# Router logits of six token tiles, computed with the router's weights stationary in four column groups

## The chip, the cores and the metric

The kernel runs on one core of a Trainium2 chip. Its engines are TensorE (PE, matrix products and transposes), VectorE (DVE), ScalarE (ACT), GpSimd (POOL) and SyncE (SP, which issues DMAs). Each runs its own instruction stream in order; they wait for each other with semaphores. The metric is device time in microseconds of one execution. A product here is written out = lhsT^T x rhs: the stationary operand lhsT (at most 128 rows by 128 columns) is loaded into PE's array, the moving operand rhs streams through, one column after another. All products in question are float32; the trace shows each as two records of MATMUL and two of LDWEIGHTS.

## What is computed

One decoder block on 1024 tokens of width 1024: a norm, a joint projection, differential attention (4 heads) beside a chunkwise mLSTM (4 heads), an output projection, then a mixture of 32 experts with 4 chosen per token, and a last norm. The part that matters:

```python
x = x + mixed @ w_out[l]
# moe(rms_norm(x, norm_ffn_g[l]), ...):
logits = (xt @ router_w + router_b).astype(jnp.float32)      # xt: 1024 x 1024, router_w: 1024 x 32
top_val, top_idx = lax.top_k(logits, TOP_K)
gates = jax.nn.softmax(top_val, axis=-1)
```

## The kernel before

The 1024 tokens are cut into NT = 8 tiles of P = 128 rows, the depth of 1024 into KD = 8 slices of 128. The kernel has three stages: the projections with the mLSTM (to some 395 us), the attention stage (to some 640 us), and the experts (a loop over 32 items with their weights streamed in, to the end).

The attention stage is a software pipeline written out by hand. A unit u = 4t + h is one head h of one tile t (N_UNITS = 32). Each engine runs a loop over u, and each of its steps holds pieces of several units:

- PE, step u: da_turn_weights(u-2, 0), the transposes of the attention weights of unit u-2 (L813); da_logit(u), the scores of unit u (L791); further transposes da_turn_weights(u-2, 1) where the tile has more than four blocks; a piece that depends on u % 4; da_values(u-2), the products with the values (L824). The piece is, with t = u//4 - 2: for u % 4 = 0 the first half of the output projection of tile t (out_project, L851), then place(t-1); for 1 its second half; for 2 turn_x1(t), the transposes of the new rows (L860); for 3 route(t), the router's logits (L870), then da_turn(t+1) (L832).
- DVE, step u: for u % 4 = 0 first da_mix(t) (L1551) and choose(t-1), which reads the logits (L1593) and picks four experts; for 1 residual (L1565), scale_rows and slots; for 3 take_h2T(t) and da_norm. Then da_combine(u-1), which joins the two exponentials of unit u-1, and da_softmax_in(u), which takes the scores of unit u out of PSUM with their maximum (L1522, L1525).
- ACT, step u: the copies of unit u-2's transposed weights out of PSUM (L1212), then pieces by u % 4, then da_exps(u), two exponentials (L1192).

da_logit(u) waits for da_max of unit u-1, that is for DVE's softmax_in(u-1), because it overwrites the banks that this reads. The PSUM banks of the pieces are dealt out in turn from a ring of two (5 and 7) by next_bank; a piece waits until the bank's last user has been read ("logits" by choose's first instruction, through logits_read).

route(t) computes 128 tokens x 32 experts: for each of the eight depth slices the 128x128 slice of h2T (the turned rows of the tile) is stationary and the 128x32 slice of the router's weights rw streams. Line 870:

```python
ins = pe.matmul(ps[:, 0:N_EXP], h2T[t % 2][:, k, :], rw[:, k, :], start=(k == 0), stop=(k == KD - 1))
```

Tiles 6 and 7 (NT-2, NT-1) are routed after the pipeline, between the last output projections. no_rows is a 128x160 tile of one constant, which POOL writes and sends to list_dram early (list_clear counts these two DMAs); nothing uses it later. The gate rows of the first stage (L659 and L664) are two products of 36 stationary columns each, into PSUM partitions 0 to 35 and 64 to 99.

Of the kernel before, what the change touches and what calls it, by code (L numbers as in the profile page):

```python
# [23 lines left out]
F32 = mybir.dt.float32  # L24
# [62 lines left out]
def build(nc, x, norm_attn_g, w_in, rel_bias_table, lambda_q1, lambda_k1, lambda_q2, lambda_k2,  # L87
# [18 lines left out]
    with ExitStack() as ctx:  # L106
# [20 lines left out]
        def kn(t, k=KD):  # L127
# [105 lines left out]
        no_rows = sb("no_rows", [P, 160], I32)  # L233
        x_idx = unit[3][:, 3136:3136 + N_EXP * LISTS].bitcast(I32)
# [13 lines left out]
         log_f_part, em_in, em_ready, cols_ps, cols_ready, wide_ps, wide_ready,  # L248
# [4 lines left out]
             "cols_ps", "cols_ready", "wide_ps", "wide_ready", "dve_step", "act_step",  # L253
# [34 lines left out]
        ident_ready, table_in, gate_w_in, lam_in_sem, router_in, squared, gain_rows_in, ml_divided, \  # L288
            ml_squared, da_squared, sum_squared = (sem(n) for n in (
            "ident_ready", "table_in", "gate_w_in", "lambda_in", "router_in", "squared",  # L290
# [4 lines left out]
        out_sent, wide_out = sem("out_sent"), sem("wide_out")  # L295
        spot_ready, last_summed = sem("spot_ready"), sem("last_summed")
# [48 lines left out]
        N_SMALL = 6 + 4  # L345
# [123 lines left out]
        def _(pool):  # L469
# [23 lines left out]
            for half in range(2):  # L493
# [4 lines left out]
                               pattern=[[1, P]], channel_multiplier=-1).then_inc(consts, 1)  # L498
            for n in range(NT):
                pool.wait_ge(mean_sq, NT + n + 1)  # L500
                pool.tensor_tensor(small[:, 4:8], small[:, 0:4], neg_half[:, 0:4], ALU.pow).then_inc(rstd_ready, 1)
# [128 lines left out]
        def _(pe):  # L630
# [50 lines left out]
            pe.wait_ge(table_in, 32)  # L681
# [182 lines left out]
            def route(t):  # L864
                pe.wait_ge(h2T_ready, 2 * t + 2)
                if t == 0:
                    pe.wait_ge(router_in, 32)
                ps = next_bank("logits", t)
                for k in range(KD):
                    ins = pe.matmul(ps[:, 0:N_EXP], h2T[t % 2][:, k, :], rw[:, k, :], start=(k == 0), stop=(k == KD - 1))  # L870
                ins.then_inc(logits_done, 1)
# [26 lines left out]
            for u in range(2, N_UNITS + 2):  # L898
                t = u // 4 - 2
                da_turn_weights(u - 2, 0)  # L900
                if u == 2:
                    ml_turn(NT - 1, next_bank("ml", NT - 1))
                if u < N_UNITS:
                    da_logit(u)
                if u + 1 < LATE_V:
                    late_values(u + 1)
                if len(da_groups[u - 2]) > 1:
                    da_turn_weights(u - 2, 1)
                if u in (6, 8):
                    turn_biases((u - 6) // 2)  # L910
                if u % 4 == 0 and t >= 0:
                    out_project(t, 0)
                    if t >= 1:
                        place(t - 1)
                if u % 4 == 1 and 0 <= t < NT - 2:
                    out_project(t, 1)
                if u % 4 == 2 and t >= 0:
                    turn_x1(t, 0)
                    turn_x1(t, 1)
                if u % 4 == 3 and t >= -1:  # L920
                    if t >= 0:
                        route(t)
                    da_turn(t + 1)
                da_values(u - 2)
# [136 lines left out]
        def _(act):  # L1061
# [22 lines left out]
            act.dma_start(table[:, :], rel_bias_table).then_inc(table_in, 16)  # L1084
            act.dma_start(one_hot, buckets).then_inc(table_in, 16)
# [120 lines left out]

            g = 0
            for u in range(len(da_units) + 2):
# [17 lines left out]
                if u % DAH == 1 and u > DAH:  # L1226
# [6 lines left out]
                    for h in range(DAH):  # L1233
                        act.activation(da_sq[:, h, :], da_o[:, h, :], ACT.Square,
                                       accum_out=small[:, h:h + 1]).then_inc(da_squared, 1)

# [73 lines left out]
        def _(dve):  # L1310
# [274 lines left out]
            def choose(t):  # L1585
# [7 lines left out]
                dve.scalar_tensor_tensor(out=lg[:, :], in0=bank(ring_bank["logits", t])[:, 0:N_EXP], scalar=rstd[:, t:t + 1],  # L1593
# [341 lines left out]
```

## Time and profile before

| what | us |
|---|---|
| median of 3 runs (lowest to highest) | 2265.82 (2259.61 to 2268.32) |
| the profiled execution | 2265.43 |
| its span, first to last instruction | 2263.6 |
| PE busy | 2192.9 |
| DVE busy | 1413.0 |
| ACT busy | 565.9 |
| POOL busy | 258.3 |

The durations below come from the profiled execution. A row of the timeline merges successive records of one form: start, time from the first start to the last end, engine, line, operation, and in brackets the idle time ahead and what ended it. The chain of the work that ended last follows the span back from its last instruction; where an engine worked without waiting, it stays on that engine.

### The profile page before, as it was taken

Reading aid. Unit: us, or ns where it says so; the run is one execution under the profiler, and the core shown is the slowest. Engines: PE = TensorE matmul, PEld = TensorE weight load, DVE = VectorE, ACT = ScalarE, POOL = GpSimd, SP = SyncE. Lnnn points to the kernel's source line nnn. Section 1 sums busy time; section 2 is a strip of 40 time slices with the busy share of each in tenths; the row PEclk is TensorE's granted clock in tenths of the full one; section 3 lists DMA queues with packets and bytes.
Section 4 is the critical chain, followed back from the end, with each engine's and each line's share of the span. In section 5 each row is a group of like instructions: output and inputs, shape, how many; then the busy total and the mean of one; then the engine's idle time right before and its main releaser. Section 6 shows DMA issues by size and latency. Waiting matters only on the chain.

```text
span 2263.6 us, 40201 instructions
## 1 busy us (share of the span) xinstructions
PE 2192.9 (97%) x14677; PEld 1893.8 (84%) x14679; DVE 1413.0 (62%) x2880; ACT 565.9 (25%) x1240; POOL 258.3 (11%) x235
## 2 busy tenths in 40 slices
PE   8999999999978999999999999999999999999996
PEld 4444554566668999999999999999999999999996
DVE  3352231678684777777778677764755566667567
ACT  2122221344311222222222222321221122222123
POOL 1000000121230110111001000110100000001013
PEclk9999999999988999999999999999999999999998
DMA  8000011210165899989989888976976788788688
GB/s 312 34 38 0 0 38 40 98 58 29 67 210 175 282 306 306 304 283 307 312 277 311 282 282 305 311 256 210 304 262 224 235 278 286 244 294 295 232 257 294
DMA packets 244662, 488.92 MB, mean 216 GB/s; under 512 B 24572, under 2 KB 24780, under 8 KB 244452
## 3 DMA queue, kind: packets, MB, share of 16 engines
q1 hardware_dynamic: 223684, 452.48, 57.3%
q0 software_dynamic: 20704, 35.60, 7.1%
q8 instruction: 34, 0.56, 0.1%
q10 hardware_dynamic: 224, 0.16, 0.0%
q14 instruction: 16, 0.13, 0.0%
HBM read 477.67 MB, written 49.63 MB: 233 GB/s over the span
## 4 chain that ended last, share of the span: by engine, by line
PE 92%; DVE 4%; issue 1%; ACT 1%; DMA 1%; POOL 0%; DVEq 0%; SPq 0%; POOLq 0%; ACTq 0%
PE PS L1024 66%; PE PS L664 15%; PE PS L851 5%; PE PS L791 1%; PE PS L824 1%; DVE pairA L1793 1%; PE PS L813 1%; PE PS L870 0%; DMA pairB<-acc_dram 0%; DVE unit L1522 0%; DVE pairA L1839 0%; PE PS L736 0%; DVE unit L1833 0%; PE PS L659 0%; PE PS L637 0%
## 5 line engine op out<-in xcount | busy, mean ns | idle before, releaser
L1024 PE MATMUL PS<-pairA,unit 128*128 x12288 | 1563.1, 290 | 31.3 <-DVE pairA L1839 11.9
L1024 PEld LDWEIGHTS PS<-pairA,unit 128*128 128x128 f32 x12288 | 1554.5, 191 | 40.0 <-issue 39.4
L1774 DVE STREAM_TRANSPOSE unit<-unit 32x512 f32<-32x512 f32 (+1 forms) x512 | 325.5, 636 | 10.3 <-DMA unit<-h_dram,cur_x 3.0
L1793 DVE STREAM_TRANSPOSE pairA<-unit 32x512 f32<-32x512 f32 (+1 forms) x512 | 325.8, 636 | 7.1
L664 PE MATMUL PS<-pairA,unit 128*128 128x512 f32 (+1 forms) x528 | 231.1, 594 | 1.4 <-issue 1.4
L1276 ACT ACTIVATE unit<-PS,cur_b 128x256 f32<-128x256 f32 x256 | 107.5, 471 | 414.9 <-PE PS L1024 414.9
L560 POOL DMA_INDIRECT unit<-h_dram,cur_x x66 | 68.8, 1042 | 1184.4 <-DVE cur_x L1829 1160.5
L664 PEld LDWEIGHTS PS<-pairA,unit 128*128 128x128 f32 (+1 forms) x528 | 97.4, 188 | 116.1 <-issue 115.4
L1259 ACT ACTIVATE unit<-unit 128x512 f32<-128x512 f32 x128 | 80.6, 630 | 453.8 <-DVE unit L1821 453.8
L1265 ACT ACTIVATE unit<-PS,cur_b 128x256 f32<-128x256 f32 x256 | 107.4, 471 | 317.7 <-PE PS L1024 314.2
L1813 DVE COPY cur_b<-b_all 128x24 f32 x32 | 6.7, 209 | 265.2 <-ACT unit L1276 261.3
L1836 DVE TENSOR_SCALAR unit<-unit 128x512 f32<-128x512 f32 x128 | 54.5, 426 | 167.0 <-ACT unit L1265 164.1
L1821 DVE TENSOR_SCALAR unit<-PS,cur_b 128x256 f32<-128x256 f32 x256 | 108.7, 478 | 40.7 <-PE PS L1024 38.6
L581 POOL DMA_INDIRECT acc_dram<-pairA,cur_y x64 | 102.8, 1606 | 211.4 <-ACT pairA L1251 201.0
L664 PE MATMUL PS<-unit,pairA 128*128 128x512 f32 x256 | 112.0, 595 | 0.3 <-ACT unit L1115 0.3
L664 PEld LDWEIGHTS PS<-unit,pairA 128*128 128x128 f32 x256 | 48.0, 190 | 59.5 <-issue 58.2
L1833 DVE TENSOR_TENSOR unit<-unit 128x512 f32<-128x512 f32 x128 | 88.4, 691 | 8.8
L1839 DVE SCALAR_TENSOR_TENSOR pairA<-unit 128x512 f32<-128x512 f32 x128 | 88.7, 693 | 4.4
L1251 ACT ACTIVATE pairA<-pairA,g_now 128x512 f32<-128x512 f32 x128 | 81.6, 715 | 1.8 <-DVE pairA L1793 1.8
L1782 DVE TENSOR_TENSOR pairA<-unit,vec 128x448 f32<-128x448 f32 x128 | 71.4, 620 | 0.0
L1522 DVE CUSTOM_DVE_ANT_0 unit<-PS,unit 128x128 f32<-128x128 f32 (+7 forms) x64 | 48.0, 750 | 29.2 <-PE PS L791 29.2
L1192 ACT ACTIVATE unit<-unit,small 128x128 f32<-128x128 f32 (+7 forms) x64 | 49.4, 772 | 51.5 <-DVE small L1525 51.0
(252 smaller groups left out, 1130.6 us busy)
## 6 DMA issues: line engine op xcount, KB each, us to landing
unit<-in_expert_w_gu_dram SPq DMA_DIRECT2D x256, 1024.0 KB, 5.1
unit<-in_expert_w_down_dram SPq DMA_DIRECT2D x128, 1024.0 KB, 8.2
unit<-in_w_in_dram SPq DMA_DIRECT2D x6, 2048.0 KB, 15.9
pairB<-in_x_dram SPq DMA_DIRECT2D x16, 512.0 KB, 5.9
unit<-in_w_out_dram SPq DMA_DIRECT2D x2, 2048.0 KB, 8.9
h_dram<-pairA SPq DMA_DIRECT2D x8, 512.0 KB, 2.6
acc_dram<-pairB SPq DMA_DIRECT2D x8, 512.0 KB
pairB<-acc_dram SPq DMA_DIRECT2D x8, 512.0 KB, 7.9
```

What stands on the lines that cost most here:

```text
L581: pool.indirect_dma_start(out=acc_dram, out_offset=bass.IndirectOffsetOnAxis(ap=cur_y[:, b:b + 1], axis=0), in_=y_rows[:, b, :], in_offset ...
L664: ins = pe.matmul(ps, lhs, rhs, start=(k == 0), stop=(k == KD - 1))
L851: ins = pe.matmul(ps, (da_mixT, ml_mixT)[k // 4][:, k % 4, P * t:P * t + P], w_o[k // 4][:, k % 4, HALF * half:HALF * half + HALF], start= ...
L1024: ins = pe.matmul(ps[:, ITEM * (j % 2):ITEM * (j % 2) + w], slot_w[s][:, k, P * j:P * j + P], xa_cols[:, ITEM * kd:ITEM * kd + KD * ITEM + ...
L1251: act.activation(half, half, ACT.Identity, scale=g_now[:, q // 2, :]).then_inc(y_evac, 1)
L1265: ins = act.activation(lin_b[:, b, ITEM * j:ITEM * j + ITEM], bank(2 + b)[:, ITEM * j:ITEM * j + ITEM], ACT.Identity, bias=cur_b[:, f:f + 1])
L1276: ins = act.activation(yT[:, 2 * s + j, :], bank(s)[:, ITEM * j:ITEM * j + ITEM], ACT.Identity, bias=cur_b[:, 2 * NF + 2 * s + j:2 * NF + ...
L1774: ins = dve.transpose(cols[:, :, :, 32 * q:32 * q + 32], rows[:, :, :, 32 * a:32 * a + 32])
L1793: ins = dve.transpose(rows[:, :, :, 32 * a:32 * a + 32], cols[:, :, :, 32 * q:32 * q + 32])
L1821: ins = dve.tensor_scalar(glu_t[:, b, ITEM * j:ITEM * j + ITEM], bank(b)[:, ITEM * j:ITEM * j + ITEM], cur_b[:, f:f + 1], LIMIT, ALU.add, ...
L1833: step.do(dve.tensor_tensor(glu_s[:, b, :], glu_t[:, b, :], glu_s[:, b, :], ALU.mult))
L1839: dve.scalar_tensor_tensor(out=actT[:, 2 * c:2 * c + 2, :].rearrange("p j n -> p (j n)"), in0=lin_c[:, b, :], scalar=1.0, in1=glu_s[:, b, ...
```

## The change

For tiles 0 to 5, route(t) exchanges the operands. The router's slice rw[:, k, :] (128x32) is now stationary, h2T[:, k, :] (128x128) streams, and the result is turned: 32 experts x 128 tokens. The eight slices go to four column groups of the array: group q (PSUM partitions 32q to 32q+31) sums slices 2q and 2q+1. So a bank holds four partial sums one below the other, 128x128 in all. ACT copies them to SBUF (take_parts, at the end of its step u = 4t + 11, behind da_exps(u)), into a part of no_rows. PE then makes one product (sum_logits, in step u = 4t + 12 between da_turn_weights(u-2, 0) and da_logit(u)): the partial sums are stationary, and a 128x32 matrix fold of four identities one below the other streams, which adds the four parts and turns the result back to tokens x experts. It goes to columns 128 to 159 of the same bank, where choose reads it. POOL makes fold after the matrix `above`. Tiles 6 and 7 stay as they were. Besides, the two loads of the bias table count to small_in rather than to a semaphore of their own, and an unused semaphore is dropped.

```diff
+        logit_parts, fold = no_rows[:, 0:P].bitcast(F32), sb("fold", [P, N_EXP])
...
-        N_SMALL = 6 + 4
+        N_SMALL = 6 + 4 + 2
...
+            step.do(pool.memset(fold[:, :], 0.0))
+            for q in range(4):
+                ins = pool.affine_select(out=fold[:, :], in_=fold[:, :], compare_op=ALU.not_equal, fill=1.0, base=-32 * q,
+                                         pattern=[[-1, N_EXP]], channel_multiplier=1)
+                if q < 3:
+                    step.do(ins)
+            ins.then_inc(consts, 1)
...
-            pe.wait_ge(table_in, 32)
...
-                for k in range(KD):
-                    ins = pe.matmul(ps[:, 0:N_EXP], h2T[t % 2][:, k, :], rw[:, k, :], start=(k == 0), stop=(k == KD - 1))
-                ins.then_inc(logits_done, 1)
+                if t >= NT - 2:
+                    for k in range(KD):
+                        ins = pe.matmul(ps[:, 0:N_EXP], h2T[t % 2][:, k, :], rw[:, k, :], start=(k == 0), stop=(k == KD - 1))
+                    ins.then_inc(logits_done, 1)
+                    return
+                for j in range(2):
+                    for q in range(4):
+                        ins = pe.matmul(ps[32 * q:32 * q + 32, 0:P], rw[:, 2 * q + j, :], h2T[t % 2][:, 2 * q + j, :],
+                                        start=(j == 0), stop=(j == 1))
+                ins.then_inc(parts_done, 1)
+
+            def sum_logits(t):
+
+                if t == 0:
+                    pe.wait_ge(consts, 6)
+                pe.wait_ge(parts_ready, t + 1)
+                pe.matmul(bank(ring_bank["logits", t])[:, P:P + N_EXP], logit_parts, fold[:, :],
+                          start=True, stop=True).then_inc(logits_done, 1)
...
+                if u % 4 == 0 and t >= 1:
+                    sum_logits(t - 1)
...
-            act.dma_start(table[:, :], rel_bias_table).then_inc(table_in, 16)
-            act.dma_start(one_hot, buckets).then_inc(table_in, 16)
+            act.dma_start(table[:, :], rel_bias_table).then_inc(small_in, 16)
+            act.dma_start(one_hot, buckets).then_inc(small_in, 16)
...
+            def take_parts(t):
+                if t == 0:
+                    act.wait_ge(list_clear, 32)
+                else:
+                    act.wait_ge(logits_done, t)
+                act.wait_ge(parts_done, t + 1)
+                act.activation(logit_parts, bank(ring_bank["logits", t])[:, 0:P], ACT.Copy).then_inc(parts_ready, 1)
...
+                if u % 4 == 3 and u >= 11:
+                    take_parts((u - 11) // 4)
...
-                dve.scalar_tensor_tensor(out=lg[:, :], in0=bank(ring_bank["logits", t])[:, 0:N_EXP], scalar=rstd[:, t:t + 1],
+                lo = P if t < NT - 2 else 0
+                dve.scalar_tensor_tensor(out=lg[:, :], in0=bank(ring_bank["logits", t])[:, lo:lo + N_EXP], scalar=rstd[:, t:t + 1],
```

On PE, the steps u = 27 and 28 (tile 4) before: the last scores of unit 27 (L791), the transposes of unit 25 (L813), the logits (L870), da_turn (L832), the values of unit 25 (L824), the transposes of unit 26, the scores of unit 28 (L791), and the output projection (L851).

```order
L791 MATMUL PS<-pairB,unit 128x384 x2
L813 MATMUL PS<-ident,unit 128x128 x3
L870 MATMUL PS<-rw,pairA 128x32 x8
L832 MATMUL PS<-ident,unit 128x128 x4
L824 MATMUL PS<-unit 128x128 x7
L813 MATMUL PS<-ident,unit 128x128 x4
L791 MATMUL PS<-pairB,unit 128x512 x4
L813 MATMUL PS<-ident,unit 128x128 x3
L851 MATMUL PS<-unit,pairA 128x512 x4
```

On PE, the same place after, with the new line numbers: L799 is da_logit, L821 da_turn_weights, L884 the products of route in column groups, L840 da_turn, L832 da_values, L893 sum_logits, L859 the output projection.

```order
L799 MATMUL PS<-pairB,unit 128x384 x2
L821 MATMUL PS<-ident,unit 128x128 x3
L884 MATMUL PS<-pairA,rw 32x128 x8
L840 MATMUL PS<-ident,unit 128x128 x4
L832 MATMUL PS<-unit 128x128 x7
L821 MATMUL PS<-ident,unit 128x128 x4
L893 MATMUL PS<-fold,no_rows 128x32
L799 MATMUL PS<-pairB,unit 128x512 x4
L821 MATMUL PS<-ident,unit 128x128 x3
L859 MATMUL PS<-unit,pairA 128x512 x4
```

The eight products keep their place with another shape, and one product stands ahead of the scores of unit 28.

On ACT, the same steps before: the copies of unit 25 (L1212), the exponentials of unit 27 (L1192), the copies of unit 26, the exponentials of unit 28.

```order
L1212 ACTIVATE unit<-PS 128x512
L1212 ACTIVATE unit<-PS 128x384
L1192 ACTIVATE unit,small<-unit,small 128x896 x2
L1212 ACTIVATE unit<-PS 128x512
L1212 ACTIVATE unit<-PS 128x384
L1192 ACTIVATE unit,small<-unit,small 128x1024 x2
```

On ACT, the same place after: L1245 are the copies, L1217 the exponentials, L1238 is take_parts.

```order
L1245 ACTIVATE unit<-PS 128x512
L1245 ACTIVATE unit<-PS 128x384
L1217 ACTIVATE unit,small<-unit,small 128x896 x2
L1238 ACTIVATE no_rows<-PS 128x128
L1245 ACTIVATE unit<-PS 128x512
L1245 ACTIVATE unit<-PS 128x384
L1217 ACTIVATE unit,small<-unit,small 128x1024 x2
```

The copy of the partial sums stands between the exponentials of unit 27 and the copies of unit 26.

## Rows read from the trace of the kernel before

**Rows 1.** The page: its head, and the shares of the last chain by engine

```profile
span 2263.6 us, 40201 instructions
...
PE 92%; DVE 4%; issue 1%; ACT 1%; DMA 1%; POOL 0%; DVEq 0%; SPq 0%; POOLq 0%; ACTq 0%
```

**Rows 2.** Stretch: length, PE, PEld, DVE, ACT, POOL busy (records), clock, DMA, GB/s

```profile
550.00:580.00 30.00, 30.00 (x149) 18.01 (x147) 22.90 (x65) 12.27 (x29) 5.05 (x5) 1.00 0.15 54
```

**Rows 3.** The last chain in order of time (start, us, what), tile 4

```profile
543.53 0.61 ACT unit L1231
...
551.64 1.71 PE PS L870 x16
...
555.38 0.44 PE PS L813 x4
...
558.21 6.87 PE PS L851 x16
```

**Rows 4.** Timeline of ACT: a 128x128 copy, then L1212 behind tiles' last exponentials

```profile
486.56 0.28 ACT L1212 ACTIVATE unit<-PS 128x128 f32<-128x128 f32 x1 [0.58 <-PE PS L813]
...
433.44 0.47 ACT L1212 ACTIVATE unit<-PS 128x384 f32<-128x384 f32 x1
...
460.93 0.57 ACT L1212 ACTIVATE unit<-PS 128x512 f32<-128x512 f32 x1
...
490.29 0.60 ACT L1212 ACTIVATE unit<-PS 128x512 f32<-128x512 f32 x1
...
522.10 0.59 ACT L1212 ACTIVATE unit<-PS 128x512 f32<-128x512 f32 x1
...
555.97 0.57 ACT L1212 ACTIVATE unit<-PS 128x512 f32<-128x512 f32 x1
...
591.83 0.58 ACT L1212 ACTIVATE unit<-PS 128x512 f32<-128x512 f32 x1
```

**Rows 5.** Timeline of PE: da_logit at u = 12 to 28, transposes at 32

```profile
432.99 1.13 PE L791 MATMUL PS<-pairB,unit 64*128 64x512 f32 x4
...
460.23 1.35 PE L791 MATMUL PS<-pairB,unit 64*128 64x512 f32 x8
...
490.18 1.56 PE L791 MATMUL PS<-pairB,unit 64*128 64x512 f32 x8
...
521.98 1.77 PE L791 MATMUL PS<-pairB,unit 64*128 64x512 f32 x8
...
555.74 1.99 PE L791 MATMUL PS<-pairB,unit 64*128 64x512 f32 x8
...
592.55 0.63 PE L813 MATMUL PS<-ident,unit 128*128 128x128 f32 x4 [1.01 <-ACT unit L1212]
```

**Rows 6.** The last chain: tiny transposes, one transpose after row-tiled scores, a 32-column product

```profile
146.54 1.08 PE PS L693 x16
...
486.26 0.26 PE PS L813
...
565.22 0.22 PE PS L879 x2
```

**Rows 7.** Timeline of PE: the gate rows, two column groups of 36 columns

```profile
77.94 0.59 PE L659 MATMUL PS<-pairA,unit 128*36 128x512 f32 x1
77.94 0.59 PE L664 MATMUL PS<-pairA,unit 128*36 128x512 f32 x1
78.37 0.59 PE L659 MATMUL PS<-pairA,unit 128*36 128x512 f32 x1
```

**Rows 8.** Timeline of DVE: reading the logits, and the residual after the first projection half

```profile
555.41 0.24 DVE L1593 SCALAR_TENSOR_TENSOR lg<-PS,rstd,rb_wide 128x32 f32<-128x32 f32 x1
...
468.68 0.69 DVE L1565 TENSOR_TENSOR pairB<-PS,pairB 128x512 f32<-128x512 f32 x1 [2.05 <-PE PS L851]
...
498.91 0.69 DVE L1565 TENSOR_TENSOR pairB<-PS,pairB 128x512 f32<-128x512 f32 x1 [2.63 <-PE PS L851]
```

**Rows 9.** Timeline of POOL: its first instruction after the constants

```profile
212.44 1.15 POOL L501 TENSOR_TENSOR small<-small,neg_half 128x4 f32<-128x4 f32 x1 [175.23 <-DVE small L1400]
```

More of the change, by code:

```diff
@@ L247, in build @@
          rstd_ready, x_scaled, x_turned, hT_ready, proj_done, proj_evac, conv_done, sig_done, qk_done,
-         log_f_part, em_in, em_ready, cols_ps, cols_ready, wide_ps, wide_ready,
+         log_f_part, em_in, em_ready, cols_ps, cols_ready, wide_ready,
          dve_step, act_step, pool_step) = (sem(n) for n in (
@@ L252, in build @@
              "proj_evac", "conv_done", "sig_done", "qk_done", "log_f_part", "em_in", "em_ready",
-             "cols_ps", "cols_ready", "wide_ps", "wide_ready", "dve_step", "act_step",
+             "cols_ps", "cols_ready", "wide_ready", "dve_step", "act_step",
              "pool_step"))
@@ L287, in build @@
             "gate_bias_clear", "pool_waited", "y_sent", "strip_spread"))
-        ident_ready, table_in, gate_w_in, lam_in_sem, router_in, squared, gain_rows_in, ml_divided, \
+        ident_ready, gate_w_in, lam_in_sem, router_in, squared, gain_rows_in, ml_divided, \
             ml_squared, da_squared, sum_squared = (sem(n) for n in (
-            "ident_ready", "table_in", "gate_w_in", "lambda_in", "router_in", "squared",
+            "ident_ready", "gate_w_in", "lambda_in", "router_in", "squared",
             "gain_rows_in", "ml_divided", "ml_squared", "da_squared",
@@ L295, in build @@
         out_sent, wide_out = sem("out_sent"), sem("wide_out")
+        parts_done, parts_ready = sem("parts_done"), sem("parts_ready")
         spot_ready, last_summed = sem("spot_ready"), sem("last_summed")
```

## The prediction

> **What bounds the kernel now.** I read four views, in this order. The page first: the span is 2263.6 us, and the chain that ended last runs 92% over TensorE (PE) [rows 1]. The changed product works only between some 400 and 640 us, so the question is which engine sets the pace there, and at which point of a tile. The table by stretches shows PE busy without a gap from 550 to 580 us, at a granted clock of 1.00, with VectorE (DVE) busy 22.90 of 30 us and ScalarE (ACT) 12.27 [rows 2]. That looks like PE alone. The chain in order of time, for the tile that is routed at 551.64, says the same: after a wait for ACT at 543.53 it stays on PE through the logits (L870, 1.71 us), da_values and da_turn_weights (555.38) and on to the output projection at 558.21 [rows 3]. Read so, each microsecond taken off the logits would be a microsecond gained.
>
> The third view, the timeline of ACT and of PE beside each other, shows how thin this is. PE goes from da_turn_weights into da_logit (L791) with next to no wait at the head of each step u = 12, 16, 20, 24, 28, at 432.99, 460.23, 490.18, 521.98 and 555.74 [rows 5]. At those moments ACT has not finished the second exponential of the unit before: it goes over to its next copy (L1212) only at 433.44, 460.93, 490.29, 522.10 and 555.97 [rows 4]. PE does not care now, since da_logit waits for DVE's maximum alone. It matters for the change, because that is where the change puts a wait.
>
> **The change, term by term.** I call the tiles 0 to 5 by the t of route(t); sum_logits(t) stands at u = 4t + 12.
>
> 1. Removed: eight products of 32 columns with 128-column weights, 1.71 us for 16 records in the chain [rows 3], so 0.107 us a record; six tiles, 10.3 us of PE.
>
> 2. Added in the same place: eight products of 128 columns with 32-column weights, 16 records, in four column groups. No row has four groups. With two groups the gate rows do overlap wholly: the two records at 77.94 run together, and the next comes 0.43 us later, what one 512-column record alone takes at the projection (6.87 us for 16 records [rows 3], 0.43 us each) [rows 7]. Lower end: four groups overlap wholly, 16/4 x 0.107 = 0.43 us. Upper end, no overlap: 1.71 us. Between them a floor of issue: 16 of the smallest records of the trace (4x4, weights 4x128) take 1.08 us [rows 6]. I take 1.08, for it is a row with as many weight loads back to back. The first full-width record after row-tiled ones takes 0.26 [rows 6] where the steady rate is 0.11 (0.44 us for four [rows 3]), so a change of tiling costs about 0.15; with two of them 1.4 us. PE's saving is then 0.3 us a tile, between zero and 1.3.
>
> 3. Added: the sum, one product of 32 columns with 128-column weights, two records: 0.22 us, as L879 [rows 6].
>
> 4. Added: ACT's copy of 128x128 out of PSUM; the same shape takes 0.28 us [rows 4].
>
> 5. Added: two waits in a row, and here the sum is decided. take_parts(t) stands behind da_exps(4t + 11) on ACT. It can't start before the exponentials of that unit, whatever PE has saved, and they wait for DVE's maximum, which waits for DVE's own combine and for a da_logit that PE ran before the logits. None of these starts earlier because the logits are shorter. sum_logits(t) waits for the copy, and behind it on PE are queued da_logit(4t + 12) and, after that, the whole output projection. So PE's saving in 1 to 3 ends as a longer wait, and PE resumes at (start of the copy on ACT) + 0.28 + 0.14 + 0.22. The 0.14 is what PE takes from the end of an ACT copy: the copy at 591.83 ends at 592.41 and PE starts at 592.55 [rows 4, 5]. The copy takes the place of L1212's starts. Together 0.64 us behind these starts:
> tile 0: 433.44 + 0.64 = 434.08 against 432.99, +1.09
> tile 1: 461.57 against 460.23, +1.34
> tile 2: 490.93 against 490.18, +0.75
> tile 3: 522.74 against 521.98, +0.76
> tile 4: 556.61 against 555.74, +0.87
> Tile 5 is another case: at u = 32 there is no da_logit, and PE waits for ACT already, until 592.55 [rows 5]. There the new copy stands ahead of L1212 on ACT and shifts it by 0.28 less the overlap of two successive instructions, about 0.09, so +0.19; the sum fits in that wait. In all **+5.0 us**.
>
> How long the column-grouped products take does not enter this sum, as long as they end in time. Before, PE reached the head of tile 3's step at 521.98 [rows 5]; now it may come until 522.52 (522.10 + 0.42). So they may take 1.71 + 0.54 = 2.2 us before they cost anything there, and somewhat more in tiles 0 and 1.
>
> Does the lateness stay? From da_logit on, PE is the chain again: projection, place, da_values, next unit, second projection. It has no reserve, and every wait inside (the DVE and ACT steps at 543.53 and its like) hangs on PE's own ends. The 5.0 us therefore reach the end of the stage; the experts' first weights are loaded behind the output projection's end, and so shift too.
>
> 6. DVE. choose(t) now waits for the sum. In tile 4 its first instruction (L1593) moves from 555.41 [rows 8] to 556.39 + 0.30 + 0.06 = 556.75, 1.34 later, and behind it stand combine and softmax_in of the unit. DVE is idle for 2.05 to 2.63 us before its next residual (L1565) in these five steps, waiting for the projection [rows 8]; that is more than 1.34, and PE asks for the later maximum only after the projection. Nothing to pay.
>
> 7. Nothing: POOL's five instructions for the fold matrix fall into its idle 175 us before 212.44 [rows 9]; the wait for the table, merged with that for the other small loads, since the same loads are issued in the same order and PE's instructions behind both waits stand next to each other; the unchanged tiles 6 and 7.
>
> **The sum.** Against the profiled run of 2265.43 us (span 2263.6, 1.8 around it; 0.4 under the median of the runs): 2265.43 + 5.0 = **2270.4 us**, 0.2% longer. A measurement of this kernel can tell about 0.5%, 11.3 us, from no change. So I forecast no measurable difference, with a sign that the profile should show.
>
> **Rivals.**
> (a) PE sets the pace after all: the copy is ready before PE asks, and the saving stays. With 1.08 us each tile gives 1.71 - 1.08 - 0.22 = 0.41, 2.5 us in all, 2262.9; with 0.43 us, 6 x 1.06 = 6.4, 2259.1. For it: the chain and the table by stretches. Against: the starts in rows 4, all behind those in rows 5. Chance 8%. The Trainium skill speaks for this side: "TensorEngine Tiling (Array Packing)", Performance Considerations, recommends for a moving operand of 32 columns to swap it with the stationary one and to tile by four columns, for up to 4x. Its 4x of 1.71 us is the lower end in 2 and gives the 2259.1; the same page warns that a copy out of PSUM may then be the bottleneck, which is where the timeline points too.
> (b) The column groups drain one another. If each of the 16 records paid the 0.15 of a changed tiling, the products take 16 x (0.107 + 0.15) = 4.1 us. Past the allowance of 2.2 us this costs about 1.9 a tile, somewhat less in tiles 0 and 1: some 9.7 us more, 2280, slower by over 0.5%. It decides from 2.2 us a tile on. Against it: the two groups at 77.94 overlap. Chance 4%. The same page states that changing the tiling mode drains TensorE; within one mode it has no such cost, so by it (b) doesn't occur.
> (c) DVE's lateness is not absorbed. It would take a step in which DVE's 2.05 us of idleness are used up; the price is at most 1.34 in five tiles, 6.7 us, 2277. Chance 7%.
> (d) The longer waits of PE let its clock fall. Waits of 1.01 us stand in the trace [rows 5] at a clock of 1.00 nearby [rows 2]. Falling from 2.4 to 1.2 GHz for one projection costs 6.87 us more, 2277. Chance 2%.
> (e) The products run one after another, 1.71 us: the change doesn't do on PE what it says. The time is that of the forecast, since it is under 2.2.
>
> **Chances.** Forecast, with (e): 79%. Range 2262 to 2277: below it reaches to (a) with 1.08 us, above to (c) and (d), and it takes in a wake-up of 0.1 to 0.5 us more per tile and the 9 us between the runs of before. Faster by over 0.5% needs more than 10.3 us of PE could give: 1%. Slower by over 0.5%: (b), half of (d): 5%. Same 94%.
>
> **What the profile after would show.** L884 (the new products) below 1.71 us per tile if the groups overlap. In PE's waits a new line, the sum (L893) on ACT's copy (L1238), six times, about 1 us each: 0.8 for the lateness plus what L884 saves. da_logit at the head of u = 12 ... 28 starts 0.64 us after the start of the copy. The stage between the first and the last output projection (L859) grows by 5 us, and nothing else does. It is wrong if those waits sum to less than what the products save, or if a DVE line grows in PE's waits, or if the products take over 2.2 us.

## The result and the profile after

| | before | after |
|---|---|---|
| median, us (lowest to highest, runs) | 2265.09 (2259.61 to 2269.23, 22) | 2284.85 (2265.38 to 2292.43, 22) |
| the profiled execution | 2265.43 | 2286.39 |
| its span | 2263.6 | 2284.5 |

The ratio is 1.0072, with a 95% interval of 1.0055 to 1.009: slower by over 0.5%, where no measurable difference was forecast. The medians lie 19.8 us apart. The times after fall into two groups with nothing between them, 7 runs from 2265.38 to 2268.21 and 15 from 2283.42 to 2292.43; where two groups mix, the median tells of the larger one (the medians' own ratio is 1.0087). The profile is of the upper group.

The page of the kernel after, its head and the shares of the chain:

```profile
span 2284.5 us, 40247 instructions
PE 90%; DVE 6%; issue 3%; ACT 1%; POOL 0%; DMA 0%; DVEq 0%; SPq 0%; POOLq 0%; ACTq 0%
```

Against [rows 1] the chain still runs over PE, with a little less of its share. The stage in question comes first. From the first output projection of the stage (L859, L851 before) to the last, before goes from 409.06 to 623.06, 214.00 us; after goes from 408.92 to 632.86, 223.94 us. So **9.9 us are lost in the attention stage**, where 5.0 were forecast, and the remaining 11 us of the span (20.9 in all) are lost behind it, where nothing was forecast. Three causes share this; each has its rows.

**First, the wait that was forecast.** PE around the sum of tile 0, by the timeline of the kernel after (start, time, engine, line, operation, in brackets the idle time ahead and what ended it), and then the other five sums:

```profile
429.48 0.65 PE L884 MATMUL PS<-pairA,rw 128*32 128x128 f32 x16
430.05 0.66 PE L840 MATMUL PS<-ident,unit 128*128 128x128 f32 x4
...
433.70 0.38 PE L893 MATMUL PS<-fold,no_rows 128*128 128x32 f32 x2 [1.77 <-ACT no_rows L1238]
...
463.91 0.41 PE L893 MATMUL PS<-fold,no_rows 128*128 128x32 f32 x2 [1.94 <-ACT no_rows L1238]
...
496.17 0.41 PE L893 MATMUL PS<-fold,no_rows 128*128 128x32 f32 x2 [1.29 <-ACT no_rows L1238]
...
528.72 0.41 PE L893 MATMUL PS<-fold,no_rows 128*128 128x32 f32 x2 [1.36 <-ACT no_rows L1238]
...
563.35 0.41 PE L893 MATMUL PS<-fold,no_rows 128*128 128x32 f32 x2 [1.48 <-ACT no_rows L1238]
...
600.08 0.41 PE L893 MATMUL PS<-fold,no_rows 128*128 128x32 f32 x2 [1.60 <-ACT no_rows L1238]
```

Six waits, 9.4 us in all, each ended by ACT's copy. The sixteen records of L884 are through in 0.57 us (429.48 to the start of the next work at 430.05), where the old form took 1.71 in tile 4 [rows 3]; the new one takes 0.58 there. ACT in the same place:

```profile
432.68 0.61 ACT L1217 ACTIVATE unit<-unit,small 128x384 f32<-128x384 f32 x1
433.20 0.19 ACT L1217 ACTIVATION_READ_ACCUMULATOR unit<-unit,small 128x1 f32 x1
433.30 0.26 ACT L1238 ACTIVATE no_rows<-PS 128x128 f32<-128x128 f32 x1
433.45 0.48 ACT L1245 ACTIVATE unit<-PS 128x384 f32<-128x384 f32 x1
```

The copy (L1238) starts when the second exponential has ended, at 433.30, and PE at 433.70. Nothing on ACT's side waits for PE's products, which had been in PSUM for three microseconds.

**Second, the clock.** By the table of stretches (stretch, then busy time of PE, PEld, DVE, ACT, POOL, then the granted clock, DMA share, GB/s), right behind three of the six waits:

```profile
434.00:436.00 2.00, 2.00 (x6) 0.50 (x5) 1.71 (x11) 0.00 (x0) 0.00 (x0) 0.54 0.00 0
...
466.00:468.00 2.00, 2.00 (x5) 0.87 (x4) 1.79 (x7) 0.00 (x0) 0.00 (x0) 0.50 0.00 0
...
602.00:604.00 2.00, 2.00 (x3) 0.69 (x3) 1.83 (x7) 0.00 (x0) 0.00 (x0) 0.50 0.03 8
```

0.50 is the lower of the two levels, 1.2 GHz. Before, all three stretches stand at 1.00; the first of them:

```profile
434.00:436.00 2.00, 2.00 (x7) 1.00 (x6) 1.79 (x10) 0.00 (x0) 0.00 (x0) 1.00 0.00 0
```

The chain of after (start, time, what) shows the price on the scores and the projection that follow:

```profile
434.08 1.90 PE PS L799 x4
435.97 7.88 PE PS L859 x16
...
464.32 1.85 PE PS L799 x8
466.17 8.14 PE PS L859 x16
...
601.28 8.56 PE PS L859 x16
```

A projection takes 6.87 to 7.08 us at full clock.

**Third, the start of the experts.** PE's timeline, the first passes of the experts' loop, of before and then of after:

```profile
652.47 18.12 PE L1024 MATMUL PS<-pairA,unit 128*128 x128 [7.59 <-issue]
679.41 18.29 PE L1024 MATMUL PS<-pairA,unit 128*128 x128 [8.82 <-DVE pairA L1839]
705.31 18.98 PE L1024 MATMUL PS<-pairA,unit 128*128 x128 [7.60 <-DVE pairA L1782]
```

```profile
662.40 0.85 PE L1049 MATMUL PS<-pairA,unit 128*128 x2 [7.81 <-issue]
665.70 18.06 PE L1049 MATMUL PS<-pairA,unit 128*128 x126 [2.44 <-issue]
698.34 0.86 PE L1049 MATMUL PS<-pairA,unit 128*128 x2 [14.59 <-issue]
701.27 19.02 PE L1049 MATMUL PS<-pairA,unit 128*128 x126 [2.07 <-issue]
725.04 5.30 PE L1049 MATMUL PS<-pairA,unit 128*128 x20 [4.74 <-issue]
```

(A pass is one turn of the experts' loop, 64 products or 128 records.) The first pass starts 9.93 us later, which is the attention stage's 9.9. By the third (705.31 and 725.04) the distance is 19.7. On the way PE stops for 2.44 and 2.07 us after the first two records of a pass of 128, with "issue" as the releaser: it waits for no engine and no transfer that the trace knows of. No row of before shows such a stop, and the change touches nothing there.

### The profile page after: what moved, and what is told of

Read it like the earlier page. It is cut to its first block, busy times and chain, and to the rows that moved or that the text cites. A ratio compares the mean times of both kernels' runs of the same rounds, so it can differ in the third digit from the quotient of the medians.

```text
span 2284.5 us, 40247 instructions
## 1 busy us (share of the span) xinstructions
PE 2197.7 (96%) x14689; PEld 1891.4 (83%) x14691; DVE 1412.6 (62%) x2880; ACT 566.7 (25%) x1246; POOL 258.7 (11%) x240
## 4 chain that ended last, share of the span: by engine, by line
PE 90%; DVE 6%; issue 3%; ACT 1%; POOL 0%; DMA 0%; DVEq 0%; SPq 0%; POOLq 0%; ACTq 0%
PE PS L1049 65%; PE PS L673 15%; PE PS L859 5%; PE PS L799 1%; DVE pairA L1830 1%; DVE unit L1558 1%; PE PS L832 1%; PE PS L821 0%; DVE pairA L1876 0%; PE PS L744 0%; DVE pairA L1618 0%; DVE unit L1870 0%; PE PS L668 0%; PE PS L646 0%; PE PS L982 0%
## 5 line engine op out<-in xcount | busy, mean ns | idle before, releaser
L1217 ACT ACTIVATE unit<-unit,small 128x128 f32<-128x128 f32 (+7 forms) x64 | 49.4, 772 | 54.4 <-DVE small L1561 53.9
```

## The experiments

All edits are to the kernel after unless they say before. Three theories are weighed in them. The wait: ACT's copy costs what was worked out, 5.0 us. The clock: it falls because PE does less and waits longer ahead of the sum, and stays up when the waiting is filled with work. The code's place: what is lost behind the stage hangs on where the code lies in memory, not on what it does. The recorded expectations call the clock's theory A and that of the place B. The rival to all three is that the products in column groups are themselves to blame.

For the theory of the code's place the program was counted. The change adds 25 instructions to PE's stream ahead of the experts' loop: 12 weight loads and 12 products (a written product is two of each) and one wait. The instruction queue of the page shows how code comes in:

```profile
q8 instruction: 33, 0.54, 0.1%
```

(packets, MB, share): 16 KB a packet. The Trainium skill, "Runtime: NRT & Kernel Launch", Instruction fetch mechanics, says the code is fetched in blocks of 16 KiB, 256 instructions, and that a taken branch whose target is not in the window present forces a fetch before execution goes on. The row's size of a packet agrees, and so does the count: two of the kernels below (the kernel after with 103 pads, and the one with the products three times and 231 pads) differ by 512 instructions and by two packets, 26 and 28. The skill's page gives no price. So a pad of 256 less 25 = 231 instructions should put the experts' loop back to the place in its block that it has in before. A pad is a count on a semaphore that nobody waits for any more, between products of the first stage:

```diff
+            pads = [231]
+            spare = ident_ready
...
+                    if kind != GATE and k < KD - 1 and pads[0] > 0:
+                        pe.sem_inc(spare, 1)
+                        pads[0] -= 1
```

I call the place of the loop in its block by what a kernel adds to before's PE stream, modulo 256: before is at 0, after at 25.

### The kernel after, again

No edit.

> The changed kernel once more, beside the others on one chip. Its times so far lie in two groups, near 2266 and near 2286 us, while the attention stage alone accounts for 5.0 us of waits (4.9 found) and 4.9 us of lowered clock. Both theories (A: the waits of PE at the sum let its granted clock fall; B: the 25 more instructions on PE move the experts' code against the 16 KB pieces in which it is fetched, and the fetches stall PE at the experts' start) expect the same here: two groups again, 2266 and 2286. If this profile is of the lower group, A expects no fall of the clock at the sum of tiles 0, 1 and 5 in it; B expects no stall after the first two records of the first two passes.

Measured: median 2287.55 us (2265.18 to 2293.05, 12 runs), ratio 1.0077 (1.0044 to 1.011). The two groups are there again, 5 runs under 2267 and 7 over 2284. This time the profile fell in the lower group, at 2265.45:

```profile
662.36 0.86 PE L1049 MATMUL PS<-pairA,unit 128*128 x2 [7.72 <-issue]
665.54 18.01 PE L1049 MATMUL PS<-pairA,unit 128*128 x126 [2.32 <-issue]
688.15 18.89 PE L1049 MATMUL PS<-pairA,unit 128*128 x128 [4.60 <-issue]
```

Up to 662.36 it is the profile of the upper group, falls of the clock at all three sums included. Then the second pass starts at 688.15, not at 698.34, and the stop inside it is missing. The theory of the place had expected both stops to be missing in the lower group; the first is still there (2.32 us). The two groups part in the first 60 us of the experts, so neither the waits nor the clock in the attention stage makes them.

### After, with 231 pads

The diff above: the place is 0.

> The changed kernel with 231 more semaphore increments on PE spread over the projections of the first stage (one between two products of 0.43 us each), so that with the 25 of the change the experts' code stands 256 instructions, 16 KB, further on than before and at the same place within such a piece. A: as the changed kernel, 2283 to 2288 in most runs, for the waits are the same. B: the stall after two records disappears at 662 and 698 us, and the time is near 2265 to 2272, with the clock's falls in the attention stage left if they are there.

Measured: 2269.95 us (2255.36 to 2280.2, 12), ratio 1.0029 (1.0009 to 1.0049); the profile is of 2276.01. 17.6 us less than the same work at place 25 on the same chip. The profiled execution is of the slower ones of this kernel; the median is only 4.0 us over before's, less than the stage costs (223.93 us, 9.9 more), for at place 0 too the times fall into groups. The stops after two records are gone, the three falls of the clock are not:

```profile
662.80 17.94 PE L1055 MATMUL PS<-pairA,unit 128*128 x128 [7.91 <-issue]
689.34 18.32 PE L1055 MATMUL PS<-pairA,unit 128*128 x128 [8.60 <-DVE pairA L1882]
715.45 14.75 PE L1055 MATMUL PS<-pairA,unit 128*128 x95 [7.79 <-DVE pairA L1825]
```

Idle times of 8.60 and 7.79 are before's 8.82 and 7.60. The theory of the code's place holds, from this side.

### Before, with 25 pads

The same edit to the kernel before, `pads = [25]`: the computation of before at the place of after.

> The kernel before with 25 more semaphore increments on PE in the projections of the first stage, which gives the experts' code the place that it has in the changed kernel, and nothing else. A: as before, 2260 to 2269. B: some 10 us slower in most runs, 2270 to 2280, with stalls after the first two records of the first two passes.

Measured: 2277.66 us (2275.36 to 2283.19, 6), ratio 1.0065 (1.0044 to 1.0086), 11.7 us over before on the same chip (2265.97, 29 runs). Its attention stage takes 213.99 us, as before, and starts 1.1 us later; of the 13.2 us between the two spans 12.1 lie behind the start of the stage's last projection. Its first passes:

```profile
654.03 0.86 PE L1030 MATMUL PS<-pairA,unit 128*128 x2 [7.88 <-issue]
657.05 18.56 PE L1030 MATMUL PS<-pairA,unit 128*128 x126 [2.16 <-issue]
690.69 0.85 PE L1030 MATMUL PS<-pairA,unit 128*128 x2 [15.08 <-issue]
693.62 19.04 PE L1030 MATMUL PS<-pairA,unit 128*128 x126 [2.07 <-issue]
```

This is after's pattern, row for row, in a kernel without the change. It holds from the other side too: 25 instructions that do nothing cost 0.65%.

### The wait alone

PE keeps the old products; the copy, the sum and their waits stay. The copy then moves old logits, and the sum's result is not used. Pads of 231: place 0.

```diff
-                if t >= NT - 2:
-                    for k in range(KD):
-                        ins = pe.matmul(ps[:, 0:N_EXP], h2T[t % 2][:, k, :], rw[:, k, :], start=(k == 0), stop=(k == KD - 1))
-                    ins.then_inc(logits_done, 1)
-                    return
-                for j in range(2):
-                    for q in range(4):
...
-                ins.then_inc(parts_done, 1)
+                for k in range(KD):
+                    ins = pe.matmul(ps[:, 0:N_EXP], h2T[t % 2][:, k, :], rw[:, k, :], start=(k == 0), stop=(k == KD - 1))
+                ins.then_inc(logits_done if t >= NT - 2 else parts_done, 1)
...
-                lo = P if t < NT - 2 else 0
+                lo = 0
```

> The changed kernel's order (ACT's copy behind the exponentials, the sum product ahead of da_logit) with the products of before, so that the wait is there and PE's saving isn't; the sum's result is not used, choose reads the old one. 231 increments are added on PE as in after_pad231, so the experts' code stands as before. PE waits about 1.1 us less at each sum (the products take 1.71 instead of 0.57). A: the clock does not fall at the sums; 2265 to 2270, 5 us over before. B alone: the same as after_pad231.

Measured: 2271.17 us (2264.19 to 2274.82, 12), ratio 1.0026 (1.0011 to 1.0041); a little above what was expected, and by time alone not to be told from the kernel with the new products at this place (2269.95). The stage is the surer reading: 409.75 to 628.73, 218.98 us, 4.98 over before, with the clock at 1.00 behind every sum. With all of the PE work of before kept, the stage pays just the forecast 5.0, and with waits of 0.27 to 1.15 us no fall of the clock follows. The theory of the wait holds, and the time of the products has no part in it.

### The copy ahead of the exponentials

ACT copies the parts before da_exps(u) instead of behind it; pads of 231, place 0.

```diff
+                if u % 4 == 3 and u >= 11:
+                    take_parts((u - 11) // 4)
                 if u < len(da_units):
                     da_exps(u)
...
-                if u % 4 == 3 and u >= 11:
-                    take_parts((u - 11) // 4)
```

> The changed kernel with take_parts ahead of da_exps(u) in ACT's step instead of behind it, so that the copy falls into ACT's idle time before the exponentials (2.1 us in tile 0, 1.6 in tile 3) and the sum finds it ready; 231 increments put the experts' code where it stood before. My account of the +5.0 us (PE waits for the copy behind the exponentials): no wait at the sum, da_logit at its old time or up to 0.8 us earlier where DVE's maximum lets it, so that the stage is 0 to 3 us shorter than before, 2259 to 2266. Rival (the wait comes from the column-grouped products themselves or from the sum, not from the place of the copy): the wait stays, 2268 to 2275. A (clock): PE waits less than 1.9 us at one place, for DVE's maximum, and the clock may still fall in tile 1.

Measured: 2262.29 us (2244.55 to 2267.84, 12), ratio 0.9986 (0.9967 to 1.0006). The stage takes 213.22 us, 0.8 less than before, and has one fall of the clock, in the step of tile 5, where its projection at 590.55 takes 8.56 us. So the same products with the same sum are no loss once the copy stands elsewhere in ACT's order.

The same edit without pads, at place 25:

> As early_copy_pad231, but without the increments, so that the experts' code stands as in the changed kernel. B (the place of the code costs by itself): 10 to 20 us slower than early_copy_pad231, with the stalls after two records at the first two passes. If the code's place costs nothing: the same as early_copy_pad231, within 3 us.

Measured: 2275.95 us (2254.64 to 2282.17, 12), ratio 1.0041 (1.0012 to 1.0069): 13.7 us more for a pad removed. The stops after two records are back:

```profile
651.74 0.86 PE L1049 MATMUL PS<-pairA,unit 128*128 x2 [7.92 <-issue]
654.82 18.23 PE L1049 MATMUL PS<-pairA,unit 128*128 x126 [2.23 <-issue]
```

### Before, with 128 pads

Half a block further: place 128.

> The kernel before with 128 increments, which moves the experts' code by half a 16 KB piece. If it is the number of added instructions that costs (25 cost 11.7 us): far more than 2277. If it is the place of a piece's edge shortly behind a jump: no gap after two records, 2258 to 2271 as before, or another gap at another place.

Measured: 2247.87 us (2247.74 to 2250.85, 6), ratio 0.993 (0.9915 to 0.9945). **Before itself becomes faster by 0.7%**, beyond the measurement's 0.5%, by instructions that do nothing: 14.9 us less than before on the same chip (2262.74, 29 runs). Its six times lie within 3.2 us. Its first passes:

```profile
655.00 18.18 PE L1030 MATMUL PS<-pairA,unit 128*128 x128 [8.82 <-issue]
673.97 16.37 PE L1030 MATMUL PS<-pairA,unit 128*128 x128 [0.79 <-issue]
690.49 32.68 PE L1030 MATMUL PS<-pairA,unit 128*128 x256 [0.15 <-issue]
```

The idle times of 8.82 and 7.60 in before, which look like part of the loop's start, are 0.79 and 0.15 here. The instruction queue, in the stretch 670 to 720 us of before, of after and of this kernel (packets, MB, share):

```profile
q8 instruction: 8, 0.13, 1.3%
```

```profile
q8 instruction: 7, 0.11, 1.0%
```

```profile
q8 instruction: 1, 0.02, 0.1%
```

Eight and seven fetches of code against one. In the first two kernels code is fetched again on the first passes of the loop, and here hardly. It doesn't go on so: from 800 to 1500 us none of the fourteen profiles has a packet of this queue, though the loop goes on turning, a pass in some 17 us. What the place costs is paid at the start of the loop.

### The column products three times over

The products of L884 are made three times (the repeats overwrite, the sum is the same): more work of PE, in what was waiting. With 103 pads (25 + 6 x 64 + 103 = 512) the place is 0.

```diff
-                for j in range(2):
-                    for q in range(4):
...
+                for rep, j, q in [(rep, j, q) for rep in range(3) for j in range(2) for q in range(4)]:
```

> The changed kernel with the eight column-grouped products made three times over, so that PE works for about 1.7 us instead of 0.57 and waits 1.1 us less at the sum; the sum itself comes no earlier or later. 103 increments put the experts' code where it stood before. A: the clock does not fall at the sums of tiles 0, 1 and 5, the stage is 5 us longer than before's and not 9.8; against after_pad231 up to 5 us faster, 2265 to 2271. If the falls have another cause than the wait: they stay.

Measured: 2272.2 us (2251.06 to 2274.3, 12), ratio 1.0012 (0.999 to 1.0035): three groups of times at this place, near 2252, 2266 and 2273, and the median falls in the uppermost, a little above the 2265 to 2271 that were expected. It told little. The stage, though, took 218.98 us, with no fall of the clock, and the same kernel at place 128 is clear (below).

### Three kernels at place 128, and one of five tiles

Since the times of before are steady at 128, the terms were weighed again there. The kernel after with 103 pads (25 + 103):

> The changed kernel with 103 increments, so that the experts' code stands as in before_pad128, whose six times lay within 3.1 us (2247.7 to 2250.9). With that place the two groups of times should vanish and the attention stage can be read alone: the 5.0 us of waits and the 4.9 us of lowered clock give 2247.9 + 9.9 = 2257.8. If the clock's falls are given back later, 2252.9.

Measured: 2257.12 us (2256.07 to 2258.15, 12), ratio 0.9969 (0.9958 to 0.998). One group. Against before at the same place +9.2 us (2247.87, but that was on another chip; the four kernels of this section ran on one chip, on which before at place 0 takes 2266.35). Its stage takes 222.26 us, +8.3, with two falls of the clock: behind the waits of 1.77 and 1.95 us, not behind that of 1.60.

The products three times, 231 pads (25 + 384 + 231 = 640):

> The column-grouped products three times over, with the experts' code in the same place as before_pad128. No falls of the clock at the sums, the wait for the copy stays: 2247.9 + 5.0 = 2252.9, so 4.9 us under after_pad103 though PE does more. If the falls don't matter to the end: as after_pad103.

Measured: 2252.94 us (2251.48 to 2254.45, 7), ratio 0.9955 (0.9939 to 0.9971). +5.1 us against before at this place on the other chip, and **4.2 us less than the kernel that makes the products once**, on the same chip and with no overlap of the times. Its timeline, its chain and its table by stretches at tile 0:

```profile
429.41 1.52 PE L889 MATMUL PS<-pairA,rw 128*32 128x128 f32 x48
...
433.63 0.38 PE L898 MATMUL PS<-fold,no_rows 128*128 128x32 f32 x2 [1.12 <-ACT no_rows L1243]
```

```profile
434.01 1.06 PE PS L805 x4
435.07 7.06 PE PS L865 x16
```

```profile
434.00:436.00 2.00, 2.00 (x8) 0.76 (x8) 1.78 (x11) 0.00 (x0) 0.00 (x0) 1.00 0.00 0
...
464.00:466.00 2.00, 2.00 (x5) 0.86 (x5) 1.79 (x9) 0.00 (x0) 0.00 (x0) 1.00 0.00 0
```

The sum starts at 433.63 as it did at 433.70: ACT decides. But PE waited 1.12 us in place of 1.77, the clock stays at 1.00, and scores and projection take 1.06 + 7.06 us in place of 1.90 + 7.88. The six waits are 4.9 us in all. The theory of the clock holds; the column groups are not to blame, for three times as many of them cost less.

The early copy, 103 pads:

> The copy ahead of the exponentials, the experts' code in the same place as before_pad128. The stage was 0.8 us shorter than before's in the padded look, with one fall of the clock (1.7 us) at tile 5: 2247.1. If the falls repeat at other places, up to 2250.

Measured: 2246.38 us (2245.12 to 2247.35, 6), ratio 0.9926 (0.9909 to 0.9944); the lowest median of all, 1.5 us below before at this place. These 1.5 us are not shown: the two ran on different chips, and their ratios to before's usual place on their own chips (0.9926 and 0.993) lie within each other's intervals. The stage is the surer reading. It takes 211.52 us, 2.5 less than before's, without a fall of the clock. PE at tile 3:

```profile
519.73 0.60 PE L827 MATMUL PS<-ident,unit 128*128 128x128 f32 x4
520.17 0.31 PE L899 MATMUL PS<-fold,no_rows 128*128 128x32 f32 x2
520.47 1.77 PE L805 MATMUL PS<-pairB,unit 64*128 64x512 f32 x8
```

No wait at the sum, and the scores start at 520.47 where before they started at 521.98 [rows 5].

The same with tile 5 routed the old way (four instructions of PE less, so 21 + 107 = 128), since PE waits there anyway:

```diff
-                if t >= NT - 2:
+                if t >= NT - 3:
...
-                if u % 4 == 0 and t >= 1:
+                if u % 4 == 0 and 1 <= t < NT - 2:
...
-                if u % 4 == 3 and u >= 11:
+                if u % 4 == 3 and 11 <= u < 31:
...
-                lo = P if t < NT - 2 else 0
+                lo = P if t < NT - 3 else 0
```

> As early_copy_pad103, with tile 5 routed by the products of before (no copy and no sum for it), 107 increments for the same place of the code. The fall of the clock at tile 5 came with PE's longest wait, which the longer products shorten by 0.9 us: if it goes, 2247.9 - 2.5 = 2245.4; if it stays, 2247.1.

Measured: 2246.94 us (2246.11 to 2247.52, 6), ratio 0.9928 (0.9911 to 0.9945), stage 211.50. No difference from the six tiles: tile 5 gives nothing, and costs nothing. The fall of the clock that this edit was to remove did not occur at place 128 with six tiles either, so of the clock it says nothing.

All medians, by kernel and place of the experts' loop:

| | place 0 | place 25 | place 128 |
|---|---|---|---|
| before | 2262.74 to 2266.35 | 2277.66 | 2247.87 |
| after | 2269.95 | 2284.85, 2287.55 | 2257.12 |
| products three times | 2272.20 | | 2252.94 |
| wait alone | 2271.17 | | |
| early copy | 2262.29 | 2275.95 | 2246.38 |
| early copy, five tiles | | | 2246.94 |

Within a column the kernels lie up to 12 us apart, within a row up to 30 (there across chips).

The medians at places 0 and 25 mix groups of times. The profiles separate the two things. Here is, for each of the fourteen, the span from the start of the stage's last projection to the end, with the packets of the instruction queue from 640 to 800 us:

| profiles | packets | us behind the stage |
|---|---|---|
| place 128, all five kernels | 6 | 1621.7 to 1623.3 |
| place 0: before, after, products three times, wait alone | 13, 14 | 1640.5 to 1643.1 |
| place 0: early copy (2245.21, of its fastest runs) | 5 | 1621.2 |
| place 25: before, after, early copy | 13, 14 | 1649.7 to 1652.7 |
| place 25: after again (lower group) | 7 | 1630.8 |

With the place and the fetches given, this time is the same within 3 us whatever the computation. So all that the wait and the clock cost is in the stage, and it reaches the end in full. Executions with few fetches are 19 to 22 us faster from there on than those with many at the same place.

## Why the prediction was wrong, point by point

**What bounds the stage** was read rightly. In the kernel after, ACT's second exponential decides when PE goes on, at each of the five heads.

**Item 2, the price of the products.** I took 1.08 us between 0.43 and 1.71; the row says 0.57. The floor of issue that I read from the 4x4 products is none for these. The forecast did not depend on it for the reason given there, but its consequence was missed (below). The Trainium skill, "TensorEngine Tiling (Array Packing)", recommends the swap with four column tiles (Performance Considerations) and puts the gain at up to 4x (Theoretical Speedup); this case shows 1.71 / 0.57 = 3.0. Its section PSUM Bottleneck, that a copy out of PSUM may then be the bottleneck, agrees with the six waits, with one restriction: the copy takes 0.26 us, and what cost was its place behind the exponentials.

**Items 4 and 5, the wait.** Right in mechanism and size. From the end of the second projection of each tile to the head of the next, after is later by 1.13, 1.42, 0.66, 0.75, 0.86 and 0.16 us, where 1.09, 1.34, 0.75, 0.76, 0.87 and 0.19 were forecast: 5.0 against 5.0. The wait alone and the products three times each make the stage 4.98 us longer. Lateness reaches the end, as said: the experts start later by what the stage loses, and at place 128 the profiled kernel with the products three times takes, behind the stage, what before takes there (1621.9 and 1621.7 us).

**Item 6, DVE,** was right: no row of DVE appears in PE's waits of the kernel after in the stage.

**Rival (d), the clock,** was the step that failed in the stage. I gave it 2%, because waits of 1.01 us stand in before at full clock. But the waits to judge were not the lateness of 0.8 to 1.3 us alone: what the products save comes on top, as item 5 says itself ("PE's saving in 1 to 3 ends as a longer wait"). They came out at 1.29 to 1.94 us, and I had compared them with 1.01; the saving alone is 1.1 us a tile and more, where item 2 had put it at 0.3. The price per fall was also too high: I took a whole projection at half clock, 6.87 us; a fall costs (1.90 - 1.06) + (7.88 - 7.06) = 1.66 us at tile 0, (1.85 - 1.28) + (8.14 - 7.06) = 1.65 at tile 1 (1.28 and 7.06 are from the chain of the kernel with the products three times), and 8.56 - 6.87 = 1.69 at tile 5. Three falls make 5.0, and with the wait's 5.0 that is the stage's 9.9. In time at place 128, where there are two falls, taking them away gave 4.2.

**The sum itself** failed most by a term that no rival named: that the edit shifts code that it doesn't touch. Item 7 put all else at nothing without asking for the instructions added to PE's stream, and "nothing else does" grow was the wrong sentence. Of the 19.8 us between the medians, 5.0 are the wait, 4 to 5 the clock, and the other 10 or so this; before with 25 pads gives it by itself as 11.7. It could have been seen that the number of PE instructions changes, and by the section of the Trainium skill cited above ("Runtime: NRT & Kernel Launch", Instruction fetch mechanics) that a jump can cost a fetch. But no row of before priced it, and even its sign was open: half a block further it gives back 14.9 us (2262.74 to 2247.87 on one chip). That the measured median lies above the range is owed to the place of the code and the clock together; at place 0 the same work has a median of 2269.95, next to the forecast by luck: there the groups of times mix so that the median is up by 4.0 us, where the stage loses 9.9.

**Rivals (a), (b), (c), (e).** (a) fell with the copy where the change puts it, and is true in part with the copy early: 2.5 us of the stage. That it isn't more is because PE then waits elsewhere: it idles 4.8 us for ACT's copies of the turned weights and 1.4 us for DVE's maxima, where in before the first of these was 3.9 and the second did not stand. (b) and (e) fell with 0.57 us. (c) did not occur.

**The signs announced.** L884 below 1.71, a line L893 on L1238 six times, da_logit 0.64 us behind the copy's start (433.30 to 434.01 is 0.71): all came. "About 1 us each" was the sign that I got wrong, at 1.57 on average, for I had put what L884 saves too low.

## What to carry to other kernels

Work taken from an engine that then waits for another is no gain, and on TensorE it can be a loss: sum the old wait, the lateness and the saving before you say that a wait is too short for the clock to fall. Where an edit changes the number of instructions ahead of a loop, compare it with the old kernel padded by as many idle instructions, and with both padded by half a block: here this decided 12 to 18 us between two places on one chip, more than any edit to the computation. A copy between two products belongs ahead of the long work in its engine's order, not behind it.

## What the runs showed of the hardware

- **The place of a loop's code.** 25 instructions that do nothing cost 11.7 us of 2266, 128 of them gained 14.9 us of 2263, and 256 more than before's count brings before's pattern back. In the bad place PE stops for 2.1 to 2.4 us after the first two products of a pass. That a jump finds its target near the end of a block, and the next block isn't there yet, would explain a stop after two products; this was argued, not shown.
- **Two or three groups of times** of one program at places 0 and 25 (after: 2265 to 2268 and 2283 to 2292), one group at place 128 (four kernels with 6 to 12 runs each, and before with 6). They part in the first 60 us of the experts' loop. With them goes the number of code fetches there: in the stretch 670 to 720 us seven packets in the upper group of after and two in the lower. Over all fourteen profiles, 5 to 7 packets from 640 to 800 us go with the fast ones and 13 or 14 with the slow ones. What decides it in a given run stays open.
- **Four column groups of float32 products** with 32 stationary columns and 128 streamed overlap to 16 records in 0.57 us, and 48 in about 1.45 (429.41 to the next work at 430.86), 0.03 to 0.04 us a record.
- **The clock.** Falls to 0.50 stood behind waits of 1.60 to 1.95 us that follow a stretch of small products, for 3 to 4 us, at 1.65 to 1.7 us each; none stood behind waits of 1.12 to 1.5 us. The border isn't sharp: the wait of 1.60 to 1.62 at tile 5 had a fall in three profiles and none in that of place 128, and with the early copy a wait of 1.86 or 1.87 at the same tile had one at places 0 and 25 and none at place 128. What makes the difference stays open.
